# Head of a transformer kernel: modulations computed slab by slab between the products of two query units, a third place for weights, c spread by transposes, fillers on TensorE up to the sums

## The reference, cut to what matters

```python
mod = (silu(c) @ w_mod + b_mod)            # for x; mod_c the same with c_ctx, for the 256 context tokens
sh1, sc1, g1, sh2, sc2, g2 = split(mod, 6)
h  = rms_norm(x, norm1_g) * (1 + sc1) + sh1
hc = rms_norm(ctx, norm1_g) * (1 + csc1) + csh1
q_a, k_a, v_a, q_b, k_b, v_b = split(h @ w_in)          # and of hc; widths 512, 128, 128, 512, 512, 512
q, k = rms_norm per head; q_a, k_a also get an axial rotary embedding
# attention, output projection, gated FFN; then a second block (gated linear attention, conv FFN)
```

## Time and profile before

| | us |
|---|---|
| median of 3 runs | 2548.23 (2548.07 to 2548.52) |
| profiled execution, whole time | 2544.92 |
| its span, first to last instruction | 2543.0 |
| TensorE busy | 2469.1 (97%) |
| VectorE, GpSimd, ScalarE busy | 1678.1, 1248.0, 1093.7 |

### The profile page before, as it was taken

One profiled execution on the slowest core, in us unless ns is written; L12 is line 12 of the kernel. 1 busy time (PEld: TensorE's weight loads), 2 busy tenths in 40 slices (PEclk: granted clock), 3 DMA queues, 4 the chain that ended last, 5 costly groups with the idle time before them and its releaser, 6 DMA issues.

```text
span 2543.0 us, 32112 instructions
## 1 busy us (share of the span) xinstructions
PE 2469.1 (97%) x11857; PEld 1985.7 (78%) x11857; DVE 1678.1 (66%) x1924; ACT 1093.7 (43%) x1746; POOL 1248.0 (49%) x735
## 2 busy tenths in 40 slices
PE   7999999999999999999999999999999999999997
PEld 5778778887778888887886777777878788887885
DVE  5674278897177656649988211234179988889988
ACT  4652467876253233334334221234244434434344
POOL 0224122673475555556876211124476655557875
PEclk9999999999999999999999999999999999999999
DMA  7462010244312222225223111011412222236221
GB/s 300 133 200 82 23 51 18 73 106 137 100 50 83 105 95 83 86 98 197 89 78 117 34 34 42 25 34 72 136 50 75 88 87 83 72 116 221 88 85 66
DMA packets 78069, 235.88 MB, mean 93 GB/s; under 512 B 8763, under 2 KB 12987, under 8 KB 77788
## 3 DMA queue, kind: packets, MB, share of 16 engines
q1 hardware_dynamic: 77916, 233.84, 27.3%
HBM read 180.59 MB, written 39.85 MB: 87 GB/s over the span
## 4 chain that ended last, share of the span: by engine, by line
PE 81%; DVE 12%; issue 3%; ACT 2%; DMA 1%; POOL 0%; SPq 0%; DVEq 0%; ACTq 0%
PE S L547 12%; PE S L548 12%; PE S L912 9%; PE S L916 9%; PE S L913 9%; PE S L950 3%; PE S L951 3%; PE S L954 3%; PE MM L784 2%; PE S L784 2%; PE S L758 2%; DVE pl L2240 1%; PE S L759 1%; PE MM L772 1%; DVE xt L1997 1%
## 5 line engine op out<-in xcount | busy, mean ns | idle before, releaser
L2563 POOL TENSOR_TENSOR wbl<-rf,wbh 128x512 fp32r<-128x512 f32 x256 | 396.5, 1555 | 248.5 <-ACT wbh L1414 248.2
L2440 POOL TENSOR_TENSOR wl<-raw,wh 128x1024 fp32r<-128x1024 f32 x58 | 146.5, 2527 | 547.0 <-ACT wh L1158 547.0
L2563 POOL TENSOR_TENSOR wbl<-wq,wbh 128x512 fp32r<-128x512 f32 (+1 forms) x168 | 276.3, 1658 | 107.4 <-ACT wbh L1414 107.4
L1414 ACT ACTIVATE wbh<-rf 128x512 fp32r<-128x512 f32 x256 | 158.4, 628 | 296.1 <-PE S L916 215.6
L912 PE MATMUL S<-th_t,wbh 128*128 128x512 f32 x640 | 251.6, 393 | 0.8 <-issue 0.6
L916 PE MATMUL S<-tl_t,wbh 128*128 128x512 f32 x640 | 251.1, 392 | 0.0
L913 PE MATMUL S<-th_t,wbl 128*128 128x512 f32 x640 | 250.5, 391 | 0.0
L547 PE MATMUL S<-hh,wh 128*128 128x512 f32 x448 | 191.3, 427 | 12.3 <-DVE gt L2371 3.7
L950 PE MATMUL S<-ph,wbh 128*128 128x512 f32 x472 | 188.8, 400 | 14.3 <-DVE xt L2142 5.9
L1414 ACT ACTIVATE wbh<-wq 128x512 fp32r<-128x512 f32 (+1 forms) x168 | 99.0, 594 | 220.8 <-PE S L954 117.4
L912 PE MATMUL S<-th_b,wbh 128*128 128x512 f32 x480 | 189.5, 395 | 2.7 <-DVE cu L2041 1.9
(11 more groups left out here) (392 smaller groups left out, 6093.0 us busy)
## 6 DMA issues: line engine op xcount, KB each, us to landing
mr<-in_w_modT SPq DMA_DIRECT2D x32, 512.0 KB, 4.6
wq<-in_w_d SPq DMA_DIRECT2D x64, 256.0 KB, 5.7
xq<-hid SPq DMA_DIRECT2D x16, 1024.0 KB, 5.1
rf<-in_w_f1g SPq DMA_DIRECT2D x22, 512.0 KB, 3.4
rf<-in_w_f1u SPq DMA_DIRECT2D x22, 512.0 KB, 3.3
hid<-pr SPq DMA_DIRECT2D x22, 512.0 KB, 2.6
rf<-in_w_f2g SPq DMA_DIRECT2D x22, 512.0 KB, 3.3
rf<-in_w_f2u SPq DMA_DIRECT2D x22, 512.0 KB, 3.3
```

Of the source, the lines that this page charges most:

```text
L1414: e.activation(flat(wbh[wslot(f, n)][:, :, :])[:, 0:x.shape[1]], x, ACT.Copy).then_inc(*w_hi.mark((f, n)))
L2440: e.tensor_tensor(l, raw[:, w % 3, 0:n], h.bitcast(F), ALU.subtract).then_inc(*w_lo.mark(w))
L2563: e.tensor_tensor(l, x, h.bitcast(F), ALU.subtract).then_inc(*w_lo.mark((f, n)))
```

## The change

- Units are in another order: 0 to 3 query a, 4 key a (`CONTEXT`), 5 to 8 key b, then as before.
- SP sends x first, its 1024 token columns alone, then the weights; the context comes as one transfer behind them. The c rows are no longer loaded: TensorE transposes `csl` columns spread over 128 columns into PSUM, and VectorE copies them to `crow`. The later rows' c is `crow[0]`, kept.
- VectorE adds seven of the eight squares, TensorE sums two tiles. Ahead of it TensorE runs 8 and 20 filler products (`idle`) on masks that VectorE now makes.
- Ten of the 16 modulation blocks (8 shifts, scales 0 and 1) are made by TensorE in a new form: `csl` is the stationary side (2 columns), 128 weight columns stream; the 2 x 128 result is copied by ScalarE (`mod_row`) and turned by a small product (`mod_turn`). Four stand before the first product, six between the products of slabs 0 to 5. Scales 2 to 7 stay row reductions on VectorE (`scale_row`), two in front of each slab's gain.
- The gain goes into ScalarE's step as its scale; VectorE's `scaled` multiplies by `rs` alone.
- The context is squared, summed, scaled and split later, during units 2 to 4. Each unit's context sums use the half `M[u % 2]`.
- Weights 2 have a third place (`wh2`, `wl2`) and need not wait for unit 0.
- `mod_rows` has 5, 5, 5, 5, 6, 6 rows behind units 3 to 8. `load_mr` comes behind `turn_unit`, row 1 waits for unit 2.

```diff
-UNITS = [("k", 0, True)] + [("k", m, False) for m in range(4)] + [("q", m, True) for m in range(4)]
+UNITS = [("q", m, True) for m in range(4)] + [("k", 0, True)] + [("k", m, False) for m in range(4)]
 UNITS += [("v", m, False) for m in range(5)] + [("q", m, False) for m in range(4)]
 NU = len(UNITS)
-ROPED, VALUES = 8, 13
+ROPED, VALUES = 4, 13
+CONTEXT = 4
+MODS = [("scale", 0), ("shift", 0), ("scale", 1)] + [("shift", _k) for _k in range(1, 8)]
+MOD_ROWS = {3: 5, 4: 5, 5: 5, 6: 5, 7: 6, 8: 6}
...
+            e.wait_ge(*d_set("masks"))
+            idle(S[j], 8)
...
+            for z in range(2):
                 for k in range(8):
+                    i = e.transpose(S[1 + z][:, 128 * k:128 * k + 128], csl[:, 2 * k + z:2 * k + z + 1].to_broadcast([128, 128]), ID)
+            i.then_inc(*turned.mark("crow"))
+            idle(S[j], 20)
+            e.wait_ge(*a_sq(("ms", 7)))
+            for r in HALF:
+                e.matmul(S[j][:, r], ONE, xq[:, 1, r], start=True, stop=False)
+            e.wait_ge(*d_acc(6))
+            for r in HALF:
+                i = e.matmul(S[j][:, r], ONE, x2h[:, r], start=False, stop=True)
+            i.then_inc(*summed.mark("ms"))
...
+            def mod_block(kind, k):
+                n = MODS.index((kind, k))
...
+                w = mod_weights(n)
+                for x in range(8):
+                    i = e.matmul(M[n % 2][0:2, 0:128], csl[:, 2 * x:2 * x + 2], w[:, 128 * x:128 * x + 128],
+                                 start=x == 0, stop=x == 7)
+                i.then_inc(*mod_made.mark(n))
...
+            def mod_turn(kind, k):
+                n = MODS.index((kind, k))
+                e.wait_ge(*a_mod(("row", n)))
+                e.wait_ge(*(mod_read(n - 2) if n >= 2 else a_ln("ms")))
...
+            mod_block("scale", 0)
+            mod_block("shift", 0)
+            mod_turn("scale", 0)
+            mod_turn("shift", 0)
+            mod_block("scale", 1)
+            mod_block("shift", 1)
+            e.wait_ge(*d_set("crow"))
+            for u in range(2):
+                SL.take(e, u, (d_ev, u))
...
             for k in range(8):
+                e.wait_ge(*a_hh(("in", k)))
+                for u in range(2):
+                    step(u, u, 8, 128, k, SL.of[u], hh, hl, parts=(0, 1))
+                if k == 0:
+                    mod_turn("scale", 1)
+                if k < 7:
+                    mod_turn("shift", k + 1)
+                if k < 6:
+                    mod_block("shift", k + 2)
+                e.wait_ge(*d_hl(("in", k)))
+                for u in range(2):
+                    i = step(u, u, 8, 128, k, SL.of[u], hh, hl, parts=(2,))
+                    if k == 7:
+                        i.then_inc(*made.mark(u))
...
                 fill = [None] * 8
-                fill[3] = lambda: unit_sums(s - 1)
+                fill[5 if s == 2 else 3] = lambda: unit_sums(s - 1)
                 if s == 2:
-                    unit_sums(0)
+                    first_sum = SL.take(e, ("sum", 0), (a_ln, 0))
+                    fill[0] = context_sums
+                    fill[1] = lambda: unit_sums(0, first_sum)
...
+                first = s == CONTEXT
+                gemm(s, s, (lambda k: a_hh(("inc", k))) if first else None, (lambda k: d_hl(("inc", k // 4))) if first else None,
+                     [(d_ev, s)], context_back(s), (hch, hcl) if cx else None, fill)
...
+                if w == 2:
+                    e.wait_ge(*d_hl(("in", 3)))
+                elif 2 <= w < FIRST["gl"] or w >= FIRST["gl"] + 3:
                     e.wait_ge(*made(w - 2))
...
-            e.activation(idb[:, :], ID, ACT.Copy)
-            e.activation(mlb[:, :], cst[:, C_ML:C_ML + 128], ACT.Copy)
...
+                    e.wait_ge(*d_acc(max(k - 3, 1)))
...
+            e.preload_act_table_set(LOG_EXP)
+            split_hi(0)
+            e.wait_ge(*summed("ms"))
+            e.activation(rs[:, 0:1024], S[SL.of["ms"]][:, :], ACT.Ln, bias=EPS).then_inc(*a_ln.mark("ms"))
+            e.activation(rs[:, 0:1024], rs[:, 0:1024], ACT.Exp, scale=-0.5).then_inc(*a_rs.mark("ms"))
             split_hi(1)
+                n = MODS.index(("shift", k))
+                e.wait_ge(*turned(("mod", n)))
+                e.activation(pair_of(M_MOD, k, 48), mod_sum("shift", k), ACT.Identity,
+                             bias=vec[:, V_BMOD + k:V_BMOD + k + 1]).then_inc(*a_mod.mark(("shift", k)))
...
+                e.activation(xw[k][:, :], xw[k][:, :], ACT.Identity, bias=mv[:, M_MOD + k:M_MOD + k + 1],
+                             scale=mv[:, M_G1 + k:M_G1 + k + 1]).then_inc(*a_aff.mark(k))
...
+                e.activation(hh[:, k, :], xw[k][:, :], ACT.Copy).then_inc(*a_hh.mark(("in", k)))
+                if k == 0:
+                    mod_row("scale", 1)
+                if k < 7:
+                    mod_row("shift", k + 1)
+                if k == 6:
+                    split_hi(2)
+                if k == 5:
+                    e.wait_ge(*l_xc(0))
+                    e.activation(flat(xcs[:, :, :]), flat(xc[:, :, :]), ACT.Square).then_inc(*a_sq.mark("msc"))
...
+            def context_in(half):
+                for k in range(4 * half, 4 * half + 4):
...
+                    e.activation(xc[:, k, :], xc[:, k, :], ACT.Identity, bias=mv[:, M_CMOD + k:M_CMOD + k + 1],
+                                 scale=mv[:, M_GC + k:M_GC + k + 1]).then_inc(*a_aff.mark(("c", k)))
+                    e.wait_ge(*a_aff(("c", k)))
+                    e.activation(hch[:, k, :], xc[:, k, :], ACT.Copy).then_inc(*a_hh.mark(("inc", k)))
...
+                if u == 0:
+                    context_root()
+                    e.preload_act_table_set("natural_log")
+                if u in (1, 2):
+                    context_in(u - 1)
...
+            for k in range(1, 7):
+                if k == 1:
...
+                e.wait_ge(*d_acc(k - 1))
+                e.tensor_tensor(x2h[:, :], x2h[:, :], xq[:, k % 3, :], ALU.add).then_inc(*d_acc.mark(k))
...
+            e.wait_ge(*turned("crow"))
+            for z in range(2):
+                i = e.tensor_copy(crow[z][:, :], S[1 + z][:, :])
...
+                e.tensor_tensor(xw[k][:, :], xw[k][:, :], rs[:, 0:1024], ALU.mult).then_inc(*d_xr.mark(k))
...
+                e.tensor_tensor_reduce(mjk[:, :], mtl[:, k, :], crow[z][:, :], 1.0, 0.0, ALU.mult, ALU.add,
+                                       mv[:, c:c + 1]).then_inc(*d_mod.mark(last[0]))
...
             scaled(0)
+            gain(0)
+            scaled(1)
+            scale_row(2, 0)
+            low(0)
+            gain(1)
+            for k in range(2, 8):
+                scaled(k)
+                if k > 2:
+                    scale_row(k, 0)
+                scale_row(k, 1)
+                gain(k)
+                low(k - 1)
+            context_squares()
+            low(7)
...
+                e.tensor_tensor(xc[:, :, :], xc[:, :, :], rs[:, 1024:1280].unsqueeze(1).to_broadcast([128, 8, 256]), ALU.mult).then_inc(*d_xr.mark("context"))
...
+                r = slice(4 * half, 4 * half + 4)
+                e.wait_ge(*a_hh(("inc", 4 * half + 3)))
+                e.tensor_tensor(hcl[:, r, :], xc[:, r, :], hch[:, r, :].bitcast(F), ALU.subtract).then_inc(*d_hl.mark(("inc", half)))
...
             def mod_rows(s):
-                for n in range(4 * s - 4, 4 * s):
+                for n in range(mod_rows_before(s), mod_rows_before(s + 1)):
                     r, c = mr[:, n % 3, :], M_RAW + 16 + n
...
             unit_take(0)
             unit_take(1)
+            context_scaled()
             unit_norm(0)
-            mod_rows(1)
             for s in range(2, NU):
                 if s >= 3:
                     unit_rope(s - 3)
                 if s < NU - 1:
                     unit_norm(s - 1)
+                if s in (3, 4):
+                    context_low(s - 3)
                 if s == NU - 1:
...
+            e.dma_start(csl[:, :], T["cc"]).then_inc(*l_const.inc(0))
...
+            for k in range(8):
+                e.dma_start(xw[k][:, :], T["xT"][k][:, 0:1024]).then_inc(*l_x.inc(k))
+            load_slab(0)
+            load_block(1)
+            load_slab(1)
+            load_block(2)
+            load_block(3)
+            for k in range(2, 8):
+                load_row(k)
+                load_block(2 + k)
+            e.dma_start(xc[:, :, :], T["xT"][:, :, 1024:1280].rearrange("a p c -> p a c")).then_inc(*l_xc.inc(0))
...
                 if n >= 3:
                     e.wait_ge(*d_mr(n - 3))
+                elif n == 1:
+                    e.wait_ge(*made(2))
...
                 if s == 5:
-                    e.wait_ge(*d_hl(("inc", 7)))
-                    e.dma_start(cb[:, :], T["c_row"].to_broadcast([128, 1024])).then_inc(*l_cb.inc(0))
+                    e.wait_ge(*d_hl(("in", 7)))
                 load_slab(s, w_lo(s - 3))
-                while n < min(32, 3 + 4 * (s - 5)):
+                if s - 6 in TURNS:
+                    turn_unit(s - 6)
```

(42 more changed lines are left out.)

272 lines of the change are left out of this document (126 added, 146 removed).

## The result

The changed kernel took 2556.33 us (median of 6 runs, 2552.32 to 2557.29), the kernel before 2548.38 (6 runs beside it, 2544.53 to 2548.82): ratio 1.0027, 95% interval 1.0017 to 1.0036. That is slower by 8 us, past the 5 us that can be told from no change. The forecast was +2.5, with "same" as its likeliest outcome (0.43, against 0.32 for "slower"); the stated range held the result. The profiled execution took 2554.14, its span 2552.3 (before 2543.0, so +9.3).

The account below looks back on a forecast made before the run. The prediction took TensorE, busy nearly everywhere after a serial head, to bound the kernel. The first product gained 27.6 us, but later waits and slow clock put the last unit at 323.8 against 321.34: +2.5, 2550.7 us, range 2540 to 2560.

Parts of the forecast that it names:

- Earlier root: Head: with x sent first, the inverse root is ready at 24.2, 21 us earlier.
- The bound of 3.4: Head: extra us the first sums would cost at half clock, putting the root at 27.6.
- First slab: Head's end: four blocks of 1.7 decide; first product at 29.4 instead of 57.04, 27.6 us gained.
- Pair stretch: Slabs of the first two units: VectorE bounds at 5.23 per slab, TensorE needs 4.6; the pair ends at 68.5.
- the ring: Pair stretch, not predicted: high parts, turn, ScalarE's three steps, next high parts wait in a circle, 5.23 us.
- Units 2 to 4: Behind the pair: waits at sum 2 and in unit 4, plus 1.7 once for slow clock; unit 4 ends at 130.2.
- the first wait: Unit 4, first low part: TensorE waits 4.8 us for a context subtraction queued behind norm(2).
- sum 2: TensorE waits 2.0 us there for the square of unit 2, delayed by ScalarE's context steps.
- the second wait: Unit 4, from slab 4: TensorE waits 8.4 us, at least 4.8, for a context subtraction behind late row reductions.
- The rest: Units 5 to 17: 193.6 us, row reductions fit, 0.56 waits go; last unit at 323.8 against 321.34.
- slower rival: Clock falls to half in the new blocks ahead of the first products: + 5.2, 2556; chance 0.18.
- faster rival: Pair stretch to unit 4: GpSimd doesn't get between, reductions 3 and 4 land in time; about 2541.5; chance 0.25.

Follow-up runs that it names:

- e2_warm_waits: Changed kernel with TensorE's two waits in unit 4 filled with 20 and 26 bf16 products: 2551.99 us.
- e10_context_between: e9_five_buffers with context steps behind the Exp of units 1 and 2, and VectorE's second context subtraction behind the take of unit 3: 2532.27 us.
- e4_no_fill: Changed kernel without the 8 and 20 filler products ahead of the first sums: 2555.37 us.
- e9_five_buffers: e1_low_early with five places for row tiles instead of three: 2535.73 us.
- e1_low_early: Changed kernel with both of VectorE's context subtractions ahead of its norm of unit 2, instead of behind the norms of units 2 and 3: 2543.45 us.
- e11_more_fill: e10_context_between with 28 filler products ahead of the first sums instead of 20: 2533.76 us.
- e6_context_after_root: Changed kernel with ScalarE's sixteen context steps together behind the root of unit 1, no longer between a unit's square and its logarithm: 2556.65 us.
- e3_rows_early: Changed kernel with VectorE's 32 row reductions starting one unit earlier: 2550.39 us.

## Why the prediction was right, and where it was wrong

1. *Earlier root*: right. Last square at 17.03 to 18.1, sums done at 21.8 (said 21.9), root 24.1 (24.2). The clock was full in this execution; in two other profiles with the same head (e2_warm_waits, e10_context_between) it was half from the middle of the sums, and the first product came 13.2 us behind the start of the sums instead of 11.5, so 1.7 later. The bound of 3.4 was met nearly in e4_no_fill (2.9).
2. *First slab*: right. Blocks 1.84 each (1.7), first product 29.67 (29.4). The gain(0), with one input in PSUM, took 0.22 beside a running GpSimd subtraction, the next VectorE step with both inputs in SBUF 2.72. By the Trainium skill ("SBUF — State Buffer", "SBUF: two separate sides") the ports shared with GpSimd are an exclusive lock, which holds up only VectorE steps with two SBUF inputs, or in a two-port mode, for the whole of the GpSimd instruction: the trace agrees.
3. *Pair stretch*: right in size (68.5 said, 69.7 measured), wrong in cause. "VectorE is the bound", TensorE 4.6: TensorE's share was undersized by 0.6 per slab (block 1.84 instead of 1.7, turn 0.31 instead of 0.2, start gaps of the products 0.3: 5.2), and there is the ring, which the prediction doesn't have. That VectorE's 5.23 came out as the period is luck in so far as the two other limits are just as long. What the prediction said would refute it, a stretch bounded by TensorE, was half true and cost little: of the 1.2 us 0.3 are the first product.
4. *Units 2 to 4*: the first wait 4.51 (4.8) and that at sum 2 1.98 (2.0) were right. The second was 5.84 (8.4, by an end at 122.5 whose terms add up to 122.3) and not of the rows' making; sum 3 ended at 117.23 instead of 112.9 and set it. Of these 4.3 us 1.5 stood already at the end of the first wait (1.2 from the pair), and 2.7 are the half clock behind it. The mis-sized term is the clock: "I add 1.7 once", measured 2.7 and 2.5. The two errors work against each other: the second wait ended 1.7 us later than said (124.22 for 122.5), and unit 4 was taken at 132.86, said 130.2.
5. *The rest*: the step "The reductions, five or six to a unit of 16.4 us, fit" failed. I added up VectorE's time and two latencies. At the sum of unit 6 (wait of 2.42) that left out that SP issues these loads behind a slab's wait and eight turn DMAs, and that reductions beside GpSimd take 3.2 us. At the sum of unit 8 (2.16) no turn DMA is involved: the six rows of unit 7 wait for one of three places each, and the norm behind them takes 3.69 us beside GpSimd instead of 1.55.

```profile
157.24 4.94 SPq L2892 DMA_DIRECT2D rp<-ka  x8
...
192.75 9.91 SPq L2879 DMA_DIRECT2D mr<-in_w_modT  x6
```
```profile
202.22 3.69 DVE L1972 SCALAR_TENSOR_TENSOR kb<-kb,mv,rs 128x1280 f32<-128x1280 f32 x1
```

The stretch took 196.8 us instead of 193.6; less the two waits it is 192.2, so the products themselves were put 1.4 too high. e9_five_buffers, with two places more and the same turn DMAs, is free of both waits: the late rows were needed for them. SP's order by itself was not tried.

Together: 1.2 at the pair's end, 1.4 more up to unit 4, 3.2 behind: 5.8 at the last unit (329.64 for 323.8), and with the forecast's 2.5 that gives the 8.3. The slower rival named 2556, and 2556.33 was measured, but that is luck: the clock in the blocks was 1.00 throughout, and the half clock came behind the waits. The faster rival looked for the waits' excess in GpSimd's lock and in late rows. The lock is in the first wait with about 2.1 of its 4.51 us (3.36 for 1.21; no kernel takes it away alone); e1_low_early shows that what mattered was the order on VectorE, which alone is worth 12.9 us by the medians and 10.3 by the score. I had written that the "low part needs context_low(0), queued behind norm(2)", and took the queue as given.

## What to carry to other kernels

A head made 27 us shorter is worth nothing if the steps that used to hide in it are queued, further on, behind something that ends late: list for each engine what stands ahead of the step that feeds the bounding engine, and whether that step's own inputs were ready. Count a wait of TensorE with the clock it costs, here about half of the wait again (2.7 us behind 4.5, and 2.5 behind 5.8). When relief of an engine changes nothing, look for a ring of waits of the same length.

## What I had not expected of the hardware

- Half clock came behind TensorE idles of 1.68 (e11_more_fill), 2.20, 2.21, 2.33 and 2.46 us, and in other executions not behind 1.68, 1.98, 2.09, 2.41, 2.42 or 2.43. It lasted 3.4 or 6.8 us (10.2 behind 11.61 in e6_context_after_root), and not by the idle's length: 3.4 behind 5.09 (e3_rows_early), 6.8 behind 4.51 and 5.84. Three passes that start within 0.59 us at full clock take 1.07 at half, so a spell costs a little under half of the part of it in which TensorE works.
- The transposes of c between the fillers: the Trainium skill ("TensorE: Matmul & The Clock Gate", "Part 4: PE-mode transpose") doesn't count them as activity. No run here decides it, since the kernel without fillers also idled 8.6 us behind them.
- VectorE steps with two SBUF inputs that started just behind a GpSimd instruction were long by a large part of it: 3.36 for 1.21, 3.19 for 1.23.
